# A decoder layer on one core: attention scores of two heads interleaved over two row halves and two PSUM banks, masks written by ScalarE, and an earlier split of the first weight panel

## What is computed

```python
h = rmsnorm(x); z = h @ w_in        # columns: u | v_A | q | k | v | gate_A | gate_B
A = gelu(u) * (tril(W_s) @ rmsnorm(gelu(v_A)) + b)           # chunks of 128
q, k = rotary(rmsnorm(q)), rotary(rmsnorm(k))                # 24 heads of 64
B = softmax-weighted sum over 3 groups of windowed attention # (window, dilation):
                                                             # (128,1), (512,4), (2048,16), 8 heads each
x += (sigmoid(gate_A)*(A @ w_oa) + sigmoid(gate_B)*(B @ w_ob)) @ w_o
x += relu(rmsnorm(x) @ w_ff1)**2 @ w_ff2                     # width 4096
x += sigmoid(rmsnorm(x) @ w_ple_gate) * (p @ w_ple_proj)
```

## Time and profile before

| | us |
|---|---|
| median of three runs | 1150.42 |
| lowest and highest | 1148.13, 1150.42 |
| the profiled execution, its whole time | 1146.99 |
| its span, first to last instruction | 1145.6 |

### The profile page before, as it was taken

One profiled execution on the slowest core, in us unless ns is written; L12 is line 12 of the kernel. 1 busy time (PEld: TensorE's weight loads), 2 busy tenths in 40 slices (PEclk: granted clock), 3 DMA queues, 4 the chain that ended last, 5 costly groups with the idle time before them and its releaser, 6 DMA issues.

```text
span 1145.6 us, 21016 instructions
## 1 busy us (share of the span) xinstructions
PE 1077.0 (94%) x8470; PEld 1055.3 (92%) x8478; DVE 720.0 (63%) x995; ACT 413.6 (36%) x707; POOL 230.9 (20%) x367
## 2 busy tenths in 40 slices
PE   4999979999999889898989999999999999999997
PEld 4998879999998779888989999999999999999996
DVE  4669977887888875999937345344443444444552
ACT  4332244444532545424226444321321331233331
POOL 2332121202230001259900111010100101102300
PEclk9999989999999999899999999999999999999998
DMA  6636734666558753448763234565555554654522
GB/s 186 204 107 201 232 131 153 197 207 194 181 176 288 195 181 125 126 147 245 207 233 111 75 99 156 169 194 191 173 192 181 191 187 159 201 193 156 167 64 79
DMA packets 131007, 196.17 MB, mean 171 GB/s; under 512 B 31984, under 2 KB 108240, under 8 KB 129136
## 3 DMA queue, kind: packets, MB, share of 16 engines
q1 hardware_dynamic: 106448, 123.54, 34.2%
q0 software_dynamic: 10112, 63.08, 16.8%
q10 hardware_dynamic: 14368, 8.46, 2.5%
HBM read 186.07 MB, written 62.00 MB: 217 GB/s over the span
## 4 chain that ended last, share of the span: by engine, by line
PE 59%; DVE 19%; POOL 7%; issue 5%; DMA 4%; ACT 3%; SPq 1%; ACTq 0%; DVEq 0%; POOLq 0%
PE gm L1016 48%; POOL kv L1769 5%; DVE w_lo L1287 3%; DVE kv L1408 3%; PE gm L992 2%; PE gm L993 2%; PE gm L994 2%; DVE fin L1328 2%; ACT w_hi L593 1%; DVE sq L1307 1%; POOL st L1739 1%; DVE acc L1455 1%; DVE kv L1449 1%; DVE st L1299 1%; PE psS L1173 1%
## 5 line engine op out<-in xcount | busy, mean ns | idle before, releaser
L1016 PE MATMUL gm<-h_hi,w_hi 128*128 128x272 f32 x1088 | 231.1, 294 | 10.3 <-DVE z L1351 4.2
L1016 PE MATMUL gm<-h_hi,w_lo 128*128 128x272 f32 x1088 | 228.1, 292 | 0.0
L1016 PE MATMUL gm<-h_lo,w_hi 128*128 128x272 f32 x1088 | 227.2, 291 | 0.0
L1287 DVE TENSOR_TENSOR w_lo<-w_raw,w_hi 128x1024 fp32r<-128x1024 f32 x150 | 178.1, 1227 | 72.7 <-ACT w_hi L593 70.8
L593 ACT CAST w_hi<-w_raw 128x1024 fp32r<-128x1024 f32 x150 | 150.3, 1048 | 152.0 <-PE gm L1016 116.5
L992 PE MATMUL gm<-w_hi,h_hi 128*128 128x256 f32 x640 | 190.0, 297 | 8.3 <-issue 8.3
L1016 PEld LDWEIGHTS gm<-h_hi,w_hi 128*128 128x128 f32 x1088 | 173.4, 191 | 12.0 <-issue 10.0
L993 PE MATMUL gm<-w_hi,h_lo 128*128 128x256 f32 x640 | 183.1, 286 | 0.0
L994 PE MATMUL gm<-w_lo,h_hi 128*128 128x256 f32 x640 | 182.4, 285 | 0.0
L1016 PEld LDWEIGHTS gm<-h_lo,w_hi 128*128 128x128 f32 x1088 | 173.8, 191 | 0.0
L1016 PEld LDWEIGHTS gm<-h_hi,w_lo 128*128 128x128 f32 x1088 | 172.9, 192 | 0.0
(11 more groups left out here) (247 smaller groups left out, 1457.3 us busy)
## 6 DMA issues: line engine op xcount, KB each, us to landing
w_raw<-in_w_ff SPq DMA_DIRECT2D x64, 512.0 KB, 5.1
out_kvs<-in_cache_kv_w POOLq DMA_DIRECT2D x64, 510.0 KB, 3.9
w_raw<-in_w_in SPq DMA_DIRECT2D x60, 512.0 KB, 5.8
kv<-in_cache_kv_w SPq DMA_DIRECT2D x128, 128.0 KB
kv<-in_cache_kv_w SPq DMA_DIRECT2D x64, 256.0 KB
out_kvs<-in_cache_kv_w POOLq DMA_DIRECT2D x32, 508.0 KB, 4.7
kv<-in_cache_kv_w POOLq DMA_DIRECT2D x128, 64.0 KB, 3.9
w_raw<-in_w_o SPq DMA_DIRECT2D x8, 512.0 KB, 4.4
```

Of the source, the lines that this page charges most:

```text
L1016: last = nc.tensor.matmul(gm[:, 2 * b2 + half, 0:HALF], w, x[:, k0 + k, half * HALF:(half + 1) * HALF], start=first, stop=end)
L1287: vec.tensor_tensor(w_lo[:, r, cols], w_raw[:, hh], w_hi[:, r, cols].bitcast(F32), ALU.subtract).then_inc(w_lo_done, 1)
```

## The change

1. The pieces of groups 0 and 1 are ordered so that pieces j and j + 1 (j even) are two heads of one pair of rows 0 to 63 and 64 to 127. PE does both in j's slot, block by block in turn, the even one in `psS` and the odd one in `gm[:, 3]`. Odd slots have no score step. Pieces of group 2 stay single, in `psS`.
2. Only the first piece of each of the two banks has its mask from a matmul. For the 30 others ACT copies the mask into the bank right after the exponential of the piece that was in it; to do so ACT waits for its own exponential. PE waits for that copy.
3. The natural units rotate over three banks of `gm`, not four, and wait for the unit three before.
4. At the start the split of panel 0 stands ahead of tile 1's high and low parts, and ahead of the third tile's squares and scaling, on ACT and on DVE.

Heads are normed and rotated on DVE as before.

```diff
-PIECES = [(0, h, b) for h in range(H) for b in range(2)] + ...
+PIECES = [(0, 2 * c + x, b) for c in range(H // 2) for b in range(2) for x in range(2)] + ...
+def paired(j):
+    return PIECES[j][0] < 2
+def score_bank(j):
+    return j % 2 if paired(j) else 0
+NEXT_IN_BANK = {j: next((x for x in range(j + 1, len(PIECES)) if score_bank(x) == score_bank(j)), None) for j in range(len(PIECES))}
+MASKED_BY_ACT = [x for x in NEXT_IN_BANK.values() if x is not None]
...
-    t, sc = TJOBS.get(s, []), SJOBS.get(s, [])
+    t, sc = TJOBS.get(s, []), [x for x in SJOBS.get(s, []) if not (paired(x[1]) and x[1] % 2)]
...
+        def s_bank(j):
+            return gm[:, 3] if score_bank(j) else psS[:]
...
-                    src = gm[0:rows, u % 4, 0:n]
+                    src = gm[0:rows, u % 3, 0:n]
...
             tile_hi(0)
+            split_hi(0, 0, None)
+            tile_hi(1)
             square_tile(2)
-            tile_hi(1)
-            split_hi(0, 0, None)
...
                     e.then_inc(exp_done, 1)
+                    act.wait_ge(exp_done, j + 1)
+                    if NEXT_IN_BANK[j] is not None:
+                        act.wait_ge(const_in, CONSTS)
+                        mk = mask_of(NEXT_IN_BANK[j])
+                        nc.scalar.copy(s_bank(j).rearrange(...), mk).then_inc(mask_written, 1)
...
-                if u >= 4:
-                    pe.wait_ge(unit_out, u - 3)
+                if u >= 3:
+                    pe.wait_ge(unit_out, u - 2)
...
             def scores(job):
-                n = SINDEX[job]
-                if n >= 1:
-                    pe.wait_ge(exp_done, n)
+                both = [j, j + 1] if paired(j) else [j]
+                for jj in both:
+                    if jj in MASKED_BY_ACT:
+                        pe.wait_ge(mask_written, MASKED_BY_ACT.index(jj) + 1)
+                    else:
+                        nc.tensor.matmul(s_bank(jj), identb[:], mask_of(jj), start=True, stop=False, skip_group_check=True)
...
+                for at, qs, ks in blocks:
+                    for jj in both:
+                        hd = PIECES[jj][1]
+                        rows, c = slice(64 * (hd % 2), 64 * (hd % 2) + 64), hd // 2
+                        last = nc.tensor.matmul(s_bank(jj)[:, at:at + 128], qT[g % 2][rows, c, qs], kT[g % 2][rows, c, ks],
+                                                start=False, stop=at == blocks[-1][0], skip_group_check=True)
+                        if at == blocks[-1][0]:
+                            last.then_inc(s_ready, 1)
...
             tile_lo(0)
+            split_lo(0, 0)
+            tile_lo(1)
             scale_tile(2)
-            tile_lo(1)
-            split_lo(0, 0)
```

More of the change, by code:

```diff
@@ L347, in build @@
         t_ready, t_out, s_ready, max_ready = sem("t_ready"), sem("t_out"), sem("s_ready"), sem("max_ready")
+        mask_written = sem("mask_written")
         exp_done, pv_ready, o_out = sem("exp_done"), sem("pv_ready"), sem("o_out")
@@ L450, in wait_heads, with mask_of @@
                 engine.wait_ge(fin_stored[n % 2], fin_count(n))
+        def s_bank(j):
+            return gm[:, 3] if score_bank(j) else psS[:]
+        def mask_of(j):
+            g, _, pair = PIECES[j]
+            return bc(masks[:, 2 + g], 1, 4) if g else bc(masks[:, 2:4], 1, 2) if pair else masks[:, 0:4]
         def x_bank(a, half):
@@ L638, in evacuate @@
                     else:
-                        nc.scalar.copy(Sn[0:NS], gm[NS:2 * NS, u % 4, 0:256]).then_inc(lo_rows, 1)
+                        nc.scalar.copy(Sn[0:NS], gm[NS:2 * NS, u % 3, 0:256]).then_inc(lo_rows, 1)
                     act.wait_ge(unit_out, u + 1)
@@ L988, in natural_unit @@
                             lh, ll = h_hi[:, k, tile], h_lo[:, k, tile]
-                            out = gm[:, u % 4, n * x:n * x + n]
+                            out = gm[:, u % 3, n * x:n * x + n]
                         wh, wl = w_hi[:, r, k * n:k * n + n], w_lo[:, r, k * n:k * n + n]
@@ L998, in natural_unit @@
                                 pe.wait_ge(h_lo_done, KD + 1)
-                            both, out = hs[k // 4][:, k % 4], gm[0:2 * NS, u % 4, 0:n]
+                            both, out = hs[k // 4][:, k % 4], gm[0:2 * NS, u % 3, 0:n]
                             nc.tensor.matmul(out, both, wh, start=k == 0, stop=False)
@@ L1153, in scores @@
                     pe.wait_ge(const_in, CONSTS)
[L1154 to L1159, removed]
+                for jj in both:
[3 more added lines that the diff above has]
+                        nc.tensor.matmul(s_bank(jj), identb[:], mask_of(jj), start=True, stop=False, skip_group_check=True)
                 if g:
[L1161 to L1164, removed]
-                else:
-                    qv = q_[rows, c].rearrange("p (c i) -> p c i", c=4)
-                    kb = k_[rows, c].rearrange("p (c i) -> p c i", c=4)
+                    blocks = [(128 * a, slice(128 * a, 128 * a + 128), slice(128 * a, 128 * a + 128)) for a in range(4)]
+                else:
+                    blocks = []
                     for x in range(2):
@@ L1170, in scores @@
                             b = 2 * pair + x
[L1171 to L1175, removed]
+                            if b - 1 + y >= 0:
+                                blocks.append((256 * x + 128 * y, slice(128 * b, 128 * b + 128), slice(128 * (b - 1 + y), 128 * (b + y))))
+                for at, qs, ks in blocks:
[6 more added lines that the diff above has]
+                            last.then_inc(s_ready, 1)
             def values(j):
```

14 lines of the change are left out of this document (8 added, 6 removed).

## The result

| | before | changed |
|---|---|---|
| median, us | 1149.32 (1148.13 to 1150.42) | 1136.18 (1134.95 to 1140.36) |
| the profiled execution, its whole time | 1146.99 | 1137.38 |
| its span | 1145.6 | 1136.0 |

The ratio is 0.9893, with an interval of 0.9871 to 0.9915: 1.1% faster, 13.1 us by the medians, 9.6 us by the two profiled executions. Before's profiled execution is 2 to 3 us under its median and the changed kernel's 1.2 us over, and the traces hold no term for that.

What follows compares the result with a forecast made beforehand. PE was taken to bind from 173 to 261 and from 410 us, DVE from 115 to 163 and 261 to 410. Terms -3.5 + 0.65 - 2.0 - 6.0 + 1.9 - 0.7 = -9.65 off 1150.4 gave 1140.8 us; range 1134 to 1149.5.

Steps and rivals of the forecast that it cites:

- Rival A: Unit 24: the clock stays up, so PE's half-rate spell behind the stall goes; 4.2 us faster, 1136.6 us; chance 0.14.
- Start: Up to unit 0: panel 0's earlier split lets unit 0 start sooner; -3.5 us (2.4 to 3.6), kept to the end.
- Three banks: Natural units: smallest margin 0.40 us, so nothing waits; cost nothing, or 1 to 2 us if DVE's reads are on the path.
- Price of a copy: ACT's mask copy: 0.65 us (0.4 to 0.9), costing only where the exponential is directly followed by a split DVE awaits.
- Rival C: Every mask copy lengthens the DVE to ACT loop, 30 x 0.65 = 19.5 us; 1157.7 us, slower; chance 0.12.
- A pair on PE: Score steps: two heads in one step save 0.86 us, up to 1.74 if the two halves' matmuls overlap.
- Rival D: Pairs: each turn between halves costs a switch, up to half of 0.40 us; 1150.5 us; chance 0.08.
- Unit 24: PE's longest stall stays, now ahead of the transposes, with less work behind it; -2.0 us, after +0.65 for an earlier copy.
- 173 to 261: Stretch from 173 to 261 us, five pairs: PE sets the end and DVE has room for 7.5 to 9.4; -6.0 us.
- rival B: From 173 to 261 us DVE and ACT bind too, so the pairs bring nothing there; 1148.1 us; chance 0.14.
- 261 to 410: Stretch from 261 to 410 us: DVE bound, pairs give nothing, three copies at panel ends cost 0.65 each; +1.9 us.
- From 410 on: From 410 us on PE bounds again and has three masks fewer at 0.23 each; -0.7 us.

Runs made afterwards that it cites:

- masks by PE: The changed kernel without ACT's mask copies, all 32 masks written by PE as before; 1135.38 us, ratio 0.989 to the kernel before.
- Start only: The kernel before with only the panel 0 split moved ahead of tile 1; 1144.97 us, ratio 0.9962 to the kernel before.
- three banks: The kernel before with only its natural units on three banks in place of four; 1148.36 us, ratio 1.001 to the kernel before.

## Why the prediction came out right, and which steps did not

The forecast was 1140.8 us; 1136.2 was measured, inside the range and 4.6 us faster than forecast. Rival A's 1136.6 is nearer, but A's cause did not happen, as said at unit 24. What held is the direction and most of the mechanism; that the terms sum up so well for the two traces is luck.

**Start.** Right: 3.71 us for a predicted 3.5. `split_hi` begins at 12.03 and `split_lo` at 13.11 and 2.36 long, in place of 14.48 and 16.83; unit 0 at 15.57. It is kept through every later stage.

**Three banks.** Right in time: nothing, alone and in the whole. In the two traces of the changed kernel the margin behind unit 50 was 0.58 and 0.14 us. That "nothing waits" is wrong in seven other traces with three banks, in which the store's wait was over 4 us and PE waited 1.03 to 1.63 us at unit 53, beside DVE's loop.

**Price of a copy.** Right in size and place. ACT, from the exponential to the next panel's split, slot 20:

```profile
140.93 0.84 ACT L892 ACTIVATE prob<-psS,ngm 128x256 f32<-128x256 f32 x2 [0.28 <-DVE ngm L1425]
141.80 0.59 ACT L899 CAST psS<-masks 128x512 f32<-128x512 bf16 x1
142.33 0.27 ACT L813 COPY O_blk<-psO 128x130 f32<-128x130 f32 x1
142.48 2.00 ACT L617 CAST w_hi<-w_raw 128x1024 fp32r<-128x1024 f32 x2
```

DVE's wait there went from 2.01 to 2.67 us: 0.66 for a predicted 0.65, and the same at slots 27, 30, 39, 42 and 57. Rival C, a copy that costs at all 30 places, is out. PE waited for a copy at 9 of its 20 score steps, 14.2 us in all, for which the sum had nothing. With masks by PE it still waits 7.8 us for exponentials at 5 of them.

**A pair on PE.** The two halves do run beside each other. With the mask, a piece cost 1.51 us, two 3.02; the pair now takes from 169.36 and one step of 0.12 to 170.66, 1.18. The saving of 1.84 is a little above the upper end, 1.74, since of the 0.40 beside the score matmuls only 1.18 - 0.89 = 0.29 us are left. The Trainium skill, TensorEngine Tiling (Array Packing), Key Properties, had said that tiles multiply in parallel, and the matmuls that start 0.01 us apart agree. Rival D, a switch in each turn, is out.

**Unit 24.** Mis-sized. The stall did move to unit 24's transposes, 2.37 us, but a second appeared in unit 23, 3.29 us, where the next pair waits for a mask copy. The stage from 18 to 25 gained 3.03 us (3.7 when run again) against a net 1.35. But not all of it is the change's. Start only and three banks have before's program there and a stall as long, 5.17 and 5.16 us, and yet the same stretch was shorter in their traces (first line start only, second three banks):

```profile
110.39:168.12 57.73, 50.30 (x379) 46.70 (x378) 47.75 (x80) 20.95 (x44) 10.85 (x14) 0.94 0.54 179
115.67:172.45 56.78, 49.84 (x379) 46.25 (x378) 47.74 (x80) 20.99 (x44) 10.85 (x14) 0.94 0.55 181
```

In before's trace TensorE stood at its lower level for 10.3 us there, in these two for 6.85, and in both traces of the changed kernel for two spells of 3.45. So the granted clock of 0.94 is no gain of the change, and rival A is not borne out; why before's spell was longer is open. Against these two traces the changed kernel gained 1.6 to 2.6 us here, and 2.3 to 3.2 when run again. On the way DVE lost 1.3 us ahead of the key mask, of which the copy explains 0.66; with start only it lost 0.5 there, and the changed kernel, run again, 0.56, so the rest stays open.

**173 to 261.** The step that failed: -6.0 forecast, -3.76 measured, though PE lost 6.65 us of work. I took PE as the bound, with room on DVE for 7.5 to 9.4 us, because DVE waited for scores for 6.2 us and for a panel's weights at the end. But only the panels from 30 and from 33, with waits of 2.18 and 0.64, got shorter by much, 2.74 and 1.46 us; the one from slot 24, with a wait of 0.47, got shorter by 0.40 (22.42 to 22.02 us), and from 27 to 30 the panel grew by the copy's 0.66. On DVE the four panels from slot 24 to 36 come to -3.94 us, beside the -3.76 seen on PE. My limit for DVE counted as reserve what was none. Most of it is the longest of the four waits for scores, 2.85 us, which lies at slot 36 ahead of the first piece of group 1 and was still 2.62 (before, then changed):

```profile
260.80 0.69 DVE L1396 TENSOR_REDUCE O<-psS 128x4 f32<-128x512 f32 x1 [2.85 <-PE psS L1163]
250.10 0.69 DVE L1424 TENSOR_REDUCE O<-psS 128x4 f32<-128x512 f32 x1 [2.62 <-PE gm L1200]
```

With it stayed the weight wait at slot 36, 1.61 us to the hundredth. Both hang on one stream of matmuls: `values` releases ACT and with it the split, and 6.6 us later (252.69 to 259.28; 6.7 in the changed kernel, 242.22 to 248.90) PE comes to the score step, so what PE gained earlier moved both ends of the wait. The rest is a lead of up to 1.9 us from unit 24. A reading was off as well: the 12.7 us of weight waits hold the 5.89 us of the stall, which was over 0.9 us behind the start of that stretch, so rival B's 82.8 us was 5 too high. Rival B, which said that DVE and ACT bind here, is right for the panels 24 to 30. PE's 99% busy in this stretch misled me: it was busy, and it was just in time.

**261 to 410.** Right in mechanism: on DVE the three copies cost 0.65, 0.65 and 0.62, and from slot 36 to 57 it is 1.55 us longer with little else changed. The whole stretch is 1.23 us longer on PE (1.68 when run again). It can't be used as proof, as kernels without the copies there had 139.9 (three banks) and 141.1 us (start only) for before's 138.18: such a stretch varies by 1 to 3 us by itself, and the store's wait and the granted clock (0.96 to 0.99) vary with it.

**From 410 on.** -0.13, -0.7 when run again, for a predicted -0.7. The tail varies from 741.5 to 745.5 us over all traces, with no relation to the edits that shows, so this is not resolved.

**The sum.** The two profiled executions differ by 9.6 us, as summed; the medians by 12.0 to 13.1. The extra 2 to 3 us come with before's profiled execution, which was that much under its median, and why was not found. So the sum matched the one pair of executions that was traced, and the prediction, taken off the median, was 4.6 us too slow.

## What to carry to other kernels

Before you credit a saving to a busy engine, measure the period of a recurring step on the next engine, panel by panel: where that period is already its own work plus waits for a third engine, the saving counts only in the panels in which it waited for the first. Moving work off the busiest engine to an idle one is no gain when the idle one stands in such a loop: here a 0.23 us matmul became a 0.65 us delay at six places, and the kernel without the copies was 0.4% faster together with a reordering; neither alone could be told from the change. A long stall of an engine is worth its length only if the engine that sets the pace waits for it. And before a gain at a stall is credited to a change, look at the same stage in a kernel that leaves it alone: here 0.5 to 1.4 of 3.0 us appeared there too.

## What the runs showed of the hardware

Sixteen 64-row matmuls of 128 columns on alternate row halves and different banks take no longer than eight, 0.89 us at full granted clock. Issued as eight and eight, the second half's still begin 0.56 us after the first's (169.65 and 170.21), when five have started: the overlap does not need strict turns, but without them most of it is lost: a pair takes 1.64 us in place of 1.09, which is 0.55 of the 0.88 us that eight of them take.

ACT's copy of 512 columns of bf16 from SBUF into PSUM takes 589 to 592 ns in all 30 cases, the same as its copy of 512 columns out of PSUM, 0.59 us. The Trainium skill, ScalarE: Activation LUTs, Step-by-step: what each stage is for, has PSUM as the faster target for ACT. These rows can't test it, as source and target are exchanged together.

DVE's panels from slot 27 on, less the one with the store's wait, repeat to 0.04 us between traces taken on different chips, with one exception, while the two spans of the changed kernel differ by 1.9 us. An effect of 0.6 us that no timing of the whole kernel could show is plain in them.
